# A fused decoder layer: the output projection as quadrant products by Strassen's scheme, on one core

## The reference

```python
D_MODEL = 2048; SEQ = 1024; BATCH = 1; DEPTH = 1

def reference(x, positions, norm_w, w_in, ..., w_out):
    h = rmsnorm(x, norm_w[layer])
    proj = jnp.einsum('bsd,dp->bsp', h, w_in[layer])
    ...
    ya = oa.reshape(b, s_len, A_WIDTH) * jax.nn.silu(ga)    # A_WIDTH = 1024
    ...
    yb = ob * jax.nn.silu(gb)                               # 1024 wide
    y = jnp.concatenate([ya, yb], axis=-1)
    x = x + jnp.einsum('bsm,md->bsd', y, w_out[layer])      # (1024 x 2048) @ (2048 x 2048)
```

## Time and profile before

| | |
|---|---|
| time, median of three runs | 1877.99 us |
| the profiled execution, first to last instruction | 1877.2 us |
| TensorE busy | 1807.0 us (96%), 8920 matmuls and transposes |
| VectorE, ScalarE, GpSimd busy | 1109.2, 799.8, 439.0 us |
| mean granted TensorE clock | 0.993 |
| DMA | 184.97 MB, mean 99 GB/s |
| an A unit, a B unit | about 117 us, about 114 us |

### The profile page before, as it was taken

One profiled execution on the slowest core, in us unless ns is written; L12 is line 12 of the kernel. 1 busy time (PEld: TensorE's weight loads), 2 busy tenths in 40 slices (PEclk: granted clock), 3 DMA queues, 4 the chain that ended last, 5 costly groups with the idle time before them and its releaser, 6 DMA issues.

```text
span 1877.2 us, 27880 instructions
## 1 busy us (share of the span) xinstructions
PE 1807.0 (96%) x8920; PEld 1507.0 (80%) x8920; DVE 1109.2 (59%) x2255; ACT 799.8 (43%) x2116; POOL 439.0 (23%) x664
## 2 busy tenths in 40 slices
PE   3899999999999999999999999999999889999999
PEld 3788878888788887888878888888888678788887
DVE  5734465665656657566575666758677866333333
ACT  5411354444544445444444444445444554222221
POOL 6512131322313223131231312313223521000000
PEclk9999999999999999999999999999999889999999
DMA  5122222222222222222222222323323544444445
GB/s 201 36 79 73 84 72 78 78 78 78 71 77 77 77 78 71 85 69 87 68 74 86 73 84 74 105 82 83 109 80 98 189 127 122 162 154 161 142 143 177
DMA packets 256504, 184.97 MB, mean 99 GB/s; under 512 B 31136, under 2 KB 227744, under 8 KB 255392
## 3 DMA queue, kind: packets, MB, share of 16 engines
q1 hardware_dynamic: 254352, 183.85, 32.3%
q10 hardware_dynamic: 2064, 0.01, 0.1%
HBM read 138.71 MB, written 45.09 MB: 98 GB/s over the span
## 4 chain that ended last, share of the span: by engine, by line
PE 79%; DVE 9%; issue 4%; DMA 3%; ACT 2%; POOL 2%; SPq 1%; DVEq 0%; ACTq 0%
PE ps_a L854 19%; PE ps_a L856 19%; PE ps_a L855 19%; PE ps_b L938 3%; PE ps_b L856 3%; PE ps_b L854 3%; PE ps_b L855 3%; PE ps_a L898 2%; DVE stage_rows L1124 2%; DMA qkv_sb<-qkv_a_dram 2%; PE ps_a L897 2%; PE ps_b L953 2%; PE ps_b L891 2%; PE ps_b L984 1%; DVE w_lo_sb L1124 1%
## 5 line engine op out<-in xcount | busy, mean ns | idle before, releaser
L854 PE MATMUL ps_a<-hT_hi,w_hi_sb 128*128 128x512 f32 x1696 | 694.1, 409 | 7.2 <-DVE stage_rows L1208 4.5
L856 PE MATMUL ps_a<-hT_hi,w_lo_sb 128*128 128x512 f32 x1696 | 667.4, 394 | 0.0
L855 PE MATMUL ps_a<-hT_lo,w_hi_sb 128*128 128x512 f32 x1696 | 664.1, 392 | 0.0
L1124 DVE TENSOR_TENSOR w_lo_sb<-w_raw_sb,w_hi_sb 128x512 fp32r<-128x512 f32 (+1 forms) x320 | 228.3, 716 | 272.1 <-ACT w_hi_sb L657 270.1
L856 PEld LDWEIGHTS ps_a<-hT_hi,w_lo_sb 128*128 128x128 f32 x1696 | 320.1, 189 | 71.8
L854 PEld LDWEIGHTS ps_a<-hT_hi,w_hi_sb 128*128 128x128 f32 x1696 | 321.2, 189 | 70.2 <-issue 7.2
L855 PEld LDWEIGHTS ps_a<-hT_lo,w_hi_sb 128*128 128x128 f32 x1696 | 321.8, 190 | 58.5
L657 ACT ACTIVATE w_hi_sb<-w_raw_sb 128x512 fp32r<-128x512 f32 (+1 forms) x320 | 197.8, 620 | 226.4 <-DMA w_raw_sb<-in_w_out 95.0
L817 ACT ACTIVATE expd<-ps_a,neg_max 128x256 f32<-128x256 f32 (+7 forms) x128 | 95.1, 743 | 213.3 <-DVE neg_max L1265 211.4
L749 ACT ACTIVATE attention_parts<-ps_b 128x512 fp32r<-128x512 f32 (+3 forms) x160 | 76.9, 521 | 224.2 <-PE ps_b L938 224.0
L1124 DVE TENSOR_TENSOR ps_a<-ps_a,mask 128x128 f32<-128x128 f32 (+2 forms) x192 | 77.5, 417 | 142.2 <-PE ps_a L898 140.8
(11 more groups left out here) (126 smaller groups left out, 2651.6 us busy)
## 6 DMA issues: line engine op xcount, KB each, us to landing
w_raw_sb<-in_w_in SPq DMA_DIRECT2D x200, 256.0 KB, 3.1
w_raw_sb<-in_w_out SPq DMA_DIRECT2D x104, 256.0 KB, 3.1
qkv_a_dram<-stage_rows SPq DMA_DIRECT2D x48, 256.0 KB, 2.4
qkv_sb<-qkv_a_dram SPq DMA_DIRECT2D x64, 192.0 KB, 3.0
x_raw_sb<-in_x SPq DMA_DIRECT2D x8, 1024.0 KB, 7.6
gates_dram<-stage_rows SPq DMA_DIRECT2D x32, 256.0 KB, 2.7
gate_y<-gates_dram SPq DMA_DIRECT2D x128, 64.0 KB, 2.4
y_dram<-gate_y SPq DMA_DIRECT2D x128, 64.0 KB, 2.3
```

Source lines behind the costliest of these rows:

```text
L854: pe.matmul(dst, a_hi, b_hi, start=start, stop=False)
L855: pe.matmul(dst, a_hi, b_lo, start=False, stop=False)
L856: return pe.matmul(dst, a_lo, b_hi, start=False, stop=stop)
L1124: return dve.tensor_tensor(o, a, b, op)
```

## The change

The output projection becomes seven products of quadrants. `y` (1024 tokens by 2048) and `w_out` (2048 by 2048) are cut in halves both ways, so a quadrant of `y` is 512 by 1024 and one of `w_out` 1024 by 1024. In Winograd's form of Strassen's scheme seven products, of sums of quadrants, replace eight. One product is 192 matmuls of 128x512.

- **Sums of weight quadrants** are made beside the A units. Twice in each A unit SyncE loads four blocks of 256 KB (`load_comb`, half steps 2 and 10), GpSimd makes four 128x512 sums from them (`combine_w`, at the end of half steps 4 and 12), SyncE stores four blocks of 256 KB (`store_comb`, half steps 6 and 14).
- **Two products under unit 11**, in place of part "O": 16 pieces of 24 matmuls, one in each half step (`early_half`). Each piece needs two weight tiles of its own, is evacuated by ScalarE, turned by four transposes (`turn_early`), copied and stored.
- **Five products behind**: 10 groups of 8 tiles, 80 tiles of 12 matmuls.
- **Sums of `y` quadrants** are made by GpSimd beside unit 11 and the tiles (`sum_1` to `sum_4`, 128x1024 each), and each product's token-side factor is split again (`z_split` on ScalarE, `z_low` on VectorE for the first, on GpSimd for the other six, 128x1024 each).
- **Joining**: the two early products come back as 4 MB (`load_g`); GpSimd adds them onto residual blocks of 128x2048 (`add_rest`, `add_gb`); VectorE's `add_group` adds the PSUM banks and waits for GpSimd (`res_ready`).

```diff
-GROUPS = [(h, n) for h in range(2) for n in (1, 2, 3)] + [(0, 0), (1, 0)]
-OUT_TILES = [(g, k) for g, (h, n) in enumerate(GROUPS) for k in range(0 if n else OK, KT)]
+NJ = 8
+EARLY = 16
+PRODUCTS = ["BB", "S2T2", "BT4", "S1T1", "S4B"]
+GROUPS = [(p, c) for p in range(len(PRODUCTS)) for c in range(2)]
+OUT_TILES = ([(0, j) for j in range(6)] + [(1, j) for j in range(6)] + [(0, 6), (0, 7), (1, 6), (1, 7)]
+             + [(g, j) for g in range(2, len(GROUPS)) for j in range(NJ)])
+REST_COUNT = {n: k + 1 for k, n in enumerate((0, 1, 2, 3, 4, 6, 5, 7))}
...
+            def load_comb(it, c):
+                wait(sp, sm["comb_stored"], it * 128 + 64 * c)
...
+                for n, src in enumerate((w_out[0, k, cols], w_out[0, k, cols2], w_out[0, kb, cols], w_out[0, kb, cols2])):
+                    sp.dma_start(w_comb[:, n, :], src).then_inc(sm["comb_in"], 16)
+            def store_comb(it, c):
+                wait(sp, sm["comb_ready"], it * 8 + (4 * c + 4))
...
+                    sp.dma_start(scr_t[t, k, cols], w_comb[:, n, :]).then_inc(sm["comb_stored"], 16)
...  SyncE, body, between load_ahead and load_step
-                    if t in (13, 14, 15, 16, 20):
-                        load_y((13, 14, 15, 16, 20).index(t))
+                    if first == len(KINDS) - 2 and s == 13:
+                        load_y_a()
+                    if first == len(KINDS) - 1 and s in (1, 2, 4):
+                        load_y_b((1, 2, 4).index(s))
+                    if 0 <= first < NJ and s % 8 == 2:
+                        load_comb(it, s // 8)
+                    if 0 <= first < NJ and s % 8 == 6:
+                        store_comb(it, s // 8)
...
                     if first == len(KINDS) and s == 3:
+                        load_g()
                         load_res(1)
+            def load_g():
...
+                for n in range(4):
...
+                    sp.dma_start(g_part[n].rearrange("p (r c) -> p r c", r=4), src).then_inc(sm["g_in"], 16)
...  TensorE
+            def early_half(m, part):
...
+                pe.wait_ge(sm["w_lo_ready"], Q + 1)
+                for k in range(4):
...
+                    mm = three(p_proj[b], w_hi[:, Q % 4, w], w_lo[:, Q % 4, w], z_hi[m // 8][:, t], z_lo[m // 8][:, t],
+                               j == 0, j == NJ - 1)
+                mm.then_inc(sm["w_used"], 1)
...  VectorE
+                    if first == len(KINDS) and s < 4:
+                        for j in range(4 * s + 4, 4 * s + 6):
+                            split_w(NQ_OUT + j, j % 4)
+                        if s == 3:
+                            add_group(0)
             def add_group(g):
+                p, c = GROUPS[g]
+                if g < len(GROUPS) - 1:
+                    dve.wait_ge(sm["w_used"], NQ_OUT + (14 + 2 * g if g < 2 else 8 * g + 8))
+                    dve.wait_ge(sm["res_ready"], REST_COUNT[n])
...
             for j in range(16, len(OUT_TILES)):
+                if j + 2 < len(OUT_TILES):
                     split_w(NQ_OUT + j + 2, (j + 2) % 4)
+                if j % 8 == 0:
+                    add_group(1 if j == 16 else j // 8 - 1)
...  GpSimd
+            def combine_w(it, c):
+                a, b, cc, d = (w_comb[:, n, :] for n in range(4))
+                wait(pool, sm["comb_in"], it * 128 + (64 * c + 64))
+                pool.tensor_tensor(d, d, b, ALU.subtract).then_inc(sm["comb_ready"], 1)
+                pool.tensor_tensor(b, b, a, ALU.subtract).then_inc(sm["comb_ready"], 1)
...
+                pool.tensor_tensor(a, a, d, ALU.add).then_inc(sm["comb_ready"], 1)
...
+                pool.tensor_tensor(cc, cc, a, ALU.subtract).then_inc(sm["comb_ready"], 1)
+            def add_rest(n):
...
+                    pool.wait_ge(res_in[n % 3], 16 * (n // 3 + 1))
+                    pool.wait_ge(sm["g_in"], 64)
...
+                pool.tensor_tensor(dst, dst, g_part[n % 2], ALU.add).then_inc(sm["res_ready"], 1)
...  GpSimd, body, behind scale_rows
+                    if 0 <= first < NJ and s % 8 == 4:
+                        combine_w(it, s // 8)
...
+                    if first == len(KINDS) and s == 2:
+                        z_low(2, 3)
+                        sum_1(3)
+                        sum_2(3)
+                        z_low(3, 0)
+                        z_low(3, 1)
+                        add_rest(0)
+                        z_low(3, 2)
+                        z_low(3, 3)
+            add_rest(1)
```

More of the change, by code:

```diff
@@ L221, in sem @@
             return ctx.enter_context(nc.semaphore(name))
+        with ExitStack() as over:
+            y_raw = [over.enter_context(nc.sbuf_tensor(name, [P, cols], F32)) for name, cols in (
+                ("y_a2_sb", 4096), ("y_gap0_sb", 8192), ("y_b1_sb", 4096), ("y_a1_sb", 4096), ("y_gap1_sb", 4096),
+                ("y_s3_sb", 4096), ("y_b2_sb", 4096))]
+            y_a2, _, y_b1, y_a1, _, y_s3, y_b2 = (a[:, :] for a in y_raw)
         hT_hi = sb("hT_hi", [P, KT, S], F32R)
@@ L233, in decoder_layer @@
             x_pieces = [x_raw_sb[:, 3 * D + j * 512:3 * D + (j + 1) * 512] for j in range(2)]
+        with nc.sbuf_tensor("g_part_sb", [P, 8 * S], F32) as g_part_sb:
+            g_part = [g_part_sb[:, c * 2048:(c + 1) * 2048] for c in range(4)]
         parts = sb("attention_parts", [P, 8, S], F32R)
@@ new lines, in _ @@
+                if j in (20, 23, 46, 54, 66):
+                    load_res((20, 23, 46, 54, 66).index(j) + 3)
+            last = len(BLOCKS) - 1
+            for r in range(4):
+                sp.wait_ge(sm["out_ready"], 4 * BLOCKS[last][0] + r + 1)
+                sp.dma_start(block_part(out2, last)[:, r], res_buf[last % 3][:, r * 512:(r + 1) * 512])\
+                  .then_inc(out_st[last % 3], 16)
+            for b in range(3):
+                sp.wait_ge(out_st[b], 16 * (len(BLOCKS[b::3]) + (3 if b == last % 3 else 0)))
@@ L1050, in body @@
                         scores_a(cur, 1, it, first)
-                    if back1 and d:
+                    if back1:
                         values(back1, it, first)
```

506 lines of the change are left out of this document (343 added, 163 removed).

## The result

The changed kernel took **1969.3 us** (median of four runs, 1966.05 to 1976.12) beside 1878.4 us before: 1.0492 times as long, 95% interval 1.0479 to 1.0504. The forecast was 1900 us, range 1848 to 1925. The sign was right, the size not: the change costs 91 us, not 22. The profiled execution has a span of 1963.9 us.

The account below looks back on a forecast made before the run. TensorE's order of work was taken as the bound; -43.5 - 18.2 + 3.7 + 2 + 53 + 22 + 3 = +22.0 on the profiled 1877.2 us, with the median 0.8 above, gave 1900 us, range 1848 to 1925.

Parts of the forecast that it names:

- Part 5: Other 60 tiles: more frequent `add_group` and VectorE splits slower beside GpSimd cost +3 us, up to 15.
- part 2: Unit 11 and tiles: idle waits and clock falls go, -18.2 us; against it transposes +3.7 and new waits +2.
- part 3: A units: weight-sum transfers ahead of the q/k/v load make TensorE wait, 6.7 us a unit, +53 us (12 to 80).
- Part 1: Output projection: 1344 matmuls instead of 1536, 192 fewer at 0.2267 us each, -43.5 us.
- Rival A: A units: step loads overtake or interleave with the 1 MB, costing 12 us instead of 53; 1859 us, chance 0.24.
- rival D: A units: GpSimd's sums delay the turned rows, `scale_rows` 4 us late, 8 x 4 us more; 1932 us, chance 0.06.
- Part 4: First output groups: VectorE's `add_group` waits for `load_g` and `add_rest`, idling TensorE before tile 18; +22 us (15 to 32).
- rival C: Tiles: bound by supply, TensorE waits about 1 us in each third tile, slower sums; 1922 us, chance 0.14.

Follow-up runs that it names:

- 8-column run: Changed kernel with nearly all GpSimd operations on y and the residual cut to 8 columns from half step 6 of unit 11 on, sums not made in full: 1918.8 us.
- run with parts: Changed kernel with GpSimd's operations on y, its splits and the residual written as operations of 256 columns, same work: 1931.0 us.

## Why the prediction was wrong, point by point

The step that failed is VectorE's work beside GpSimd. Part 5 priced it as a fixed surcharge of 0.9 us on some splits (+3 us in the tiles), and part 2 put it at nothing in unit 11. The runs show a split held until GpSimd's operation ends, up to 5.09 us instead of 0.69: 23 us in the tiles and 15 in unit 11. Next to it part 3 had the right mechanism and too small a size, 53 where 75 were measured.

**Part 1, fewer matmuls, -43.5.** Right. Pace and count hold: in the 8-column run the tiles take 243.1 us, 217.6 by pace, 14.8 the wait ahead of tile 16, the rest the end, smaller waits and the slow clock.

**Part 2, waits that go, and unit 11.** Right once GpSimd is out of the way: the forecast gives 111.5 + 12.2 = 123.7 us, the run with parts takes 120.6. In the changed kernel it was 135.6. The step that failed is "new waits in unit 11 ... I take +2 us": it priced ScalarE's work and GpSimd's place ahead of `scale_probs`, not what GpSimd's 17 operations of 1024 columns there do to VectorE. That is 15 us.

**Part 3, A units, +53.** The right place, queue and half steps, and TensorE waits there as described; the sum came to 75, inside its bounds of 12 to 80. Three terms were too small. The delay in half step 6 to 7 was 2.7 where 3.3 were measured: the choice took issues or bytes, the larger of the two, and both count, for the load is first issued late and then lands late. In half step 11 I had a wait of 1.75 us and no fall of the clock; the eight waits there were 2.32 to 3.75 us, 2.9 in the mean, and the clock fell behind seven of them. The last term is that clock. The waits at `turn_qk` for `qkv_a` grew from 7.1 to 56.5, by 49.4; the junction's wait of 4.50, which I had kept, became one of 2.80 behind `load_y_a`, -1.7; what is left of 75.1, 27.4 us or 3.4 a unit, is the slow clock, where I had 1.74, with 0.5 for VectorE. TensorE's busy time in a unit bears that out: 114.9 to 115.0 us before, 115.1 in the one without a fall, 117.9 to 119.4 in the six others that were measured from `turn_qk` to `turn_qk`. Rival A fell with it, rival D was refuted by the run without sums.

The Trainium skill ("DMA: Bandwidth & Descriptors", Queues, rings and completion order) says that descriptors are consumed in ring order, and this half of its rule fits the step load: it landed after 4.2 us behind 1 MB, after 2.3 behind an eighth of it.

**Part 4, first groups, +22.** The size came out (19.88 us and a slow start; 15 to 32), the row of it did not. I had the wait ahead of tile 18 with tiles 14 to 17 as cover, 13.1 us and then 3.1 more. It stands ahead of tile 16, since that tile needs the bank of group 0, with 14 and 15 alone as cover (5.4 us instead of 10.9), and no second wait for a bank follows (4.8 us with its slow start). Two errors of opposite sign cancelled, so that the size came out is luck. `load_g` took 13.6 us (forecast 14), `add_rest(0)` 4.49 (forecast 3.8). The 4497 ns of the Trainium skill ("GPSIMD Engine Reference", Elementwise) for 2048 columns was the better figure.

**Part 5, the other tiles, +3.** This is the other large miss, and rival C's mechanism at more than its price. The row of 1.61 us in the earlier trace rows was read as a surcharge of 0.9 us for "beside GpSimd". It was a subtraction held by a GpSimd operation that was itself short: the third of the 5.14 us row ran from 1469.64 to 1471.35, the split from 1470.16 to 1471.77. The surcharge is the rest of that operation, up to 4.4 us beside the new ones of 2048 columns. Tiles 257.5 with parts against 280.7: 23 us. Two waits that the forecast had nowhere are still in the tiles with parts: 3.84 us at 1708.58 for GpSimd's `z_low`, and 4.92 at 1754.49 for `w_lo`, behind the split that was held for 3.52.

The sum of the misses: 22 in the A units and the junction, 12 in unit 11 and 31 in the tiles, 65 of the 69 us between 1900 and 1969; the rest is how the profiled execution stands to the median.

## What to carry to other kernels

Before work is given to GpSimd beside a VectorE that feeds TensorE, list VectorE's operations with two SBUF operands: each can last as long as the longest GpSimd operation beside it, so GpSimd's should be short pieces (256 columns here), even where the sum of the pieces is larger, or the time of the feeder must stand in the forecast at that length. A bulk transfer goes behind the latency-bound load of its half step, never ahead: the same 32 MB cost 79 us or nothing that could be seen. A wait of TensorE costs more than its length where the clock falls behind it: here 27 us on top of 48 of waits. Where a sum frees a bank, the summand that comes late is added last.
